# A DeltaNet and sliding-window layer: block stores from two queues, a block load that the queue waits for, and new places in the schedule

## The reference

```
g = cumsum(-exp(a_log) * softplus(a + dt_bias))
a_mat = strict(k_beta k^T) * decay
t_mat = inverse(I + a_mat)              # the triangular inverse
v_new = t_mat (v_beta - k_beta e^g S);  o = q e^g S + (q k^T * decay) v_new
S = S * e^g_tot + k_dec^T v_new
y = concat(rmsnorm(o) * silu(z), attention * silu(z_b)) @ w_out
out = LayerNorm(2^0.25 * x + y)
```

## Time and profile before

| | |
|---|---|
| median of 3 runs (lowest to highest) | 1247.62 us (1246.43 to 1248.07) |
| profiled execution, its own time | 1249.48 us |
| its span, first to last instruction | 1247.7 us |
| PE busy | 1149.6 us (92%) |
| DVE busy | 650.1 us (52%) |
| ACT busy | 505.5 us (41%) |
| POOL busy | 198.0 us (16%) |
| granted TensorE clock, mean | 0.970 |
| DMA engines' mean share | 45%, 147 GB/s |

### The profile page before, as it was taken

How to read it: one execution, slowest core, us unless ns; L and a number is a source line. 1 busy time by engine, 2 the same in 40 slices (tenths; PEclk the granted TensorE clock), 3 DMA queues, 4 the chain that set the end, 5 groups by cost and what they waited for, 6 DMA issues and landing times. The chain is left out here.

```text
span 1247.7 us, 19748 instructions
## 1 busy us (share of the span) xinstructions
PE 1149.6 (92%) x7340; PEld 900.9 (72%) x7340; DVE 650.1 (52%) x1996; ACT 505.5 (41%) x1475; POOL 198.0 (16%) x268
## 2 busy tenths in 40 slices
PE   4988989888999999999999999999899989899997
PEld 2766767666777868786786878777686868687776
DVE  3345554645355464646356364745437363636565
ACT  3363636363352625353352433336233534353220
POOL 4522323122210101023000101012100000000340
PEclk9998989898999999999999999999999999999999
DMA  6753745545572543632436362625244343522232
GB/s 212 287 191 123 252 164 161 179 136 153 161 237 102 164 160 104 211 127 78 150 132 193 124 192 79 201 84 172 85 165 157 110 137 110 168 79 61 94 109 84
DMA packets 63887, 183.57 MB, mean 147 GB/s; under 512 B 16240, under 2 KB 28976, under 8 KB 50480
## 3 DMA queue, kind: packets, MB, share of 16 engines
q1 hardware_dynamic: 63792, 182.32, 44.1%
HBM read 138.22 MB, written 44.07 MB: 146 GB/s over the span
## 5 line engine op out<-in xcount | busy, mean ns | idle before, releaser
L760 PE MATMUL bank<-xr,w 128*128 128x512 f32 x2496 | 684.8, 414 | 5.1 <-ACT conv_in L1091 3.2
L760 PEld LDWEIGHTS bank<-xr,w 128*128 128x128 f32 x2496 | 455.5, 193 | 108.5 <-issue 14.8
L733 POOL TENSOR_TENSOR x_tile<-x_tile,gain 128x256 f32<-128x256 f32 x40 | 28.1, 736 | 716.6 <-DVE x_tile L1484 716.6
L810 PE MATMUL bank<-wo,y_split 128*128 128x512 f32 x432 | 118.8, 409 | 0.0
L810 PEld LDWEIGHTS bank<-wo,y_split 128*128 128x128 f32 x432 | 76.2, 188 | 17.1 <-issue 1.9
L1410 DVE SCALAR_TENSOR_TENSOR kq<-conv_in,convw_all,kq 128x512 f32<-128x512 f32 x96 | 76.5, 796 | 3.4
L1332 ACT ACTIVATE blocks<-bank 128x128 f32<-128x128 f32 x64 | 17.8, 277 | 149.0 <-PE bank L1027 148.8
L1605 DVE TENSOR_TENSOR y_step<-blocks,y_cols 128x60 f32<-128x60 f32 (+14 forms) x240 | 49.7, 207 | 49.7 <-DMA blocks<-n_spill 42.0
L1227 ACT ACTIVATE score<-score,neg_max 128x256 f32<-128x256 f32 (+1 forms) x128 | 62.5, 490 | 16.8 <-DVE neg_max L1572 16.8
L1297 ACT ACTIVATE blocks<-bank 128x256 f32<-128x256 f32 (+1 forms) x64 | 24.4, 382 | 105.1 <-PE bank L974 73.7
L1692 DVE SCALAR_TENSOR_TENSOR t<-bank,cols_all,v_tok 128x128 f32<-128x128 f32 x64 | 22.3, 348 | 84.8 <-PE bank L1012 84.8
(11 more groups left out here) (214 smaller groups left out, 1762.1 us busy)
## 6 DMA issues: line engine op xcount, KB each, us to landing
w<-w_split SPq DMA_DIRECT2D x78, 1024.0 KB, 5.0
w_split<-w SPq DMA_DIRECT2D x26, 1024.0 KB, 4.9
blocks<-n_spill SPq DMA_DIRECT2D x16, 512.0 KB
y_spill<-y_out SPq DMA_DIRECT2D x30, 256.0 KB, 6.3
y_tile<-w_in SPq DMA_DIRECT2D x13, 512.0 KB, 6.1
x_tile<-w_in SPq DMA_DIRECT2D x13, 512.0 KB, 6.2
y_tile<-y_spill SPq DMA_DIRECT2D x12, 512.0 KB, 6.7
x_tile<-x SPq DMA_DIRECT2D x12, 512.0 KB, 5.6
```

The costliest lines, as they stand in the source:

```text
L733: nc.gpsimd.tensor_tensor(res[:, part], res[:, part], gain[:, part], ALU.mult).then_inc(scaled.sem, 1)
L760: ins = nc.tensor.matmul(bank[at % 2][:], w[:, turn % 3, wp, k, :], xr[:, xp, k], start=(step == 0), stop=(step == 3 * KT - 1))
L810: ins = nc.tensor.matmul(bank[at % 2][:], y_place(t)[:, yp, k], wo[:, k, wp, half * UNIT:(half + 1) * UNIT], start=(step == 0), stop=(step ...
```

## The change

1. `store_blocks` on SP issues five of the eight block stores; ACT issues the other three, after its squares of q and a wait for all of `n_t`.
2. `load_blocks(n)` comes directly after SP's stores, ahead of `load_decay(n + 1)`, and SP then waits for the blocks' landing before anything further (`load_x(s + 1, 3)`, weight loads, spills).
3. On ACT `eg_row` is made before the squares of k instead of after. A weight split (`w_hi`) that falls on a slot's last job is held until after ACT's block stores.
4. `silu` stands before chunk 2's square (the third chunk) instead of chunk 3's, where the gates are ready by then: in short and middle slots with n < 15. In long slots it stays.
5. In middle slots the job order is o0, bz, o1 instead of o0, o1, bz. `split_y` of the next tile moves from chunk 2 to chunk 3.
6. Places: `AT_VTOK` (L948) 0.13 to 0.16; `first` 0.47, 0.36, 0.42 to 0.49, 0.375, 0.44 (short, long, middle); `step0` and `step` as in the diff.

```diff
+SP_BLOCKS = 5
     if s == 1 or s == 2:
-        return ["q", "k", "v", "z", "o0", "o1", "bz", "bq"]
+        return ["q", "k", "v", "z", "o0", "bz", "o1", "bq"]
-AT_SCORES0, AT_VTOK, AT_TURNS0, AT_VALUES0 = 0.09, 0.13, 0.24, 0.31
+AT_SCORES0, AT_VTOK, AT_TURNS0, AT_VALUES0 = 0.09, 0.16, 0.24, 0.31
-        first = 0.47 if short else 0.36 if long else 0.42
+        first = 0.49 if short else 0.375 if long else 0.44
-        self.step0, self.step = (0.665, 0.082) if short else (0.6, 0.097) if long else (0.62, 0.092)
+        self.step0, self.step = (0.685, 0.077) if short else (0.605, 0.096) if long else (0.635, 0.088)
@@ sync
-                for g in range(P // BASE):
+                for g in range(SP_BLOCKS):
                 store_blocks(n)
+                load_blocks(n)
                 if i < AH - 1:
                     after(sp, pt_ready, n, 2)
                     load_decay(n + 1)
+                after(sp, blocks_in, n, 16)
                 if i == AH - 1 and 0 < s < SBS - 1:
                     after(sp, x_low_dve, s + 1, 1)
                     load_x(s + 1, 3)
-                load_blocks(n)
@@ scalar
+            held = []
+            def split_weight():
+                while held:
+                    w_hi(held.pop())
                 if at in W_AT and W_AT[at] + 3 < TILES_W:
-                    w_hi(W_AT[at] + 3)
+                    if at + 1 < len(JOBS) and JOBS[at + 1].n > max(job.n, -1) >= 0:
+                        held.append(W_AT[at] + 3)
+                    else:
+                        w_hi(W_AT[at] + 3)
             def slot(n):
+                after(act, g_row_in, n, 16)
+                after(act, resid_ready, n - 1, CH)
+                nc.scalar.activation(eg_row[:], decay[:], ACT.Exp).then_inc(eg_ready.sem, 1)
                 after(act, ktok_done, n, 1)
...
+                after(act, n_ready, n, CH)
+                for g in range(SP_BLOCKS, P // BASE):
+                    part = slice(g * BASE, (g + 1) * BASE)
+                    act.dma_start(n_spill[n, g].rearrange("t a c -> a t c"), n_t[part, :, part]).then_inc(n_stored.sem, 16)
+                split_weight()
                 after(act, small, n, 3)
...
-                after_jobs(n, at.step0)
+                after_jobs(n, min(at.step0, 0.66))
                 copy_turned(n, 1)
+                silu_before = CH - 2 if silu_at(n) - n < at.chunk(CH - 2) and n < SLOTS - 1 else CH - 1
                 for c in range(CH):
+                    if c == silu_before:
+                        after_jobs(n, max(at.chunk(c), silu_at(n) - n))
+                        if c < CH - 1:
+                            silu(n, True)
                     if c == CH - 1:
...
-                        silu(n, True)
+                        if silu_before == c:
+                            silu(n, True)
@@ vector
-                    if c == 2:
+                    if c == CH - 1:
                         if t is not None and i == AH - 2:
                             split_y(t + 1)
```

More of the change, by code:

```diff
@@ L1252, in slot @@
                 nc.scalar.activation(r_k[:], ln_ss[:, 0], ACT.Exp, scale=-0.5).then_inc(rk_ready.sem, 1)
-                after(act, g_row_in, n, 16)
-                after(act, resid_ready, n - 1, CH)
-                nc.scalar.activation(eg_row[:], decay[:], ACT.Exp).then_inc(eg_ready.sem, 1)
                 if i == 0:
@@ L1316, in slot @@
                 take(y_inv[low, :, high], half_tiles(bank[7])[low], 9)
-                after_jobs(n, at.step0)
+                after_jobs(n, min(at.step0, 0.66))
                 copy_turned(n, 1)
+                silu_before = CH - 2 if silu_at(n) - n < at.chunk(CH - 2) and n < SLOTS - 1 else CH - 1
                 for c in range(CH):
+                    if c == silu_before:
+                        after_jobs(n, max(at.chunk(c), silu_at(n) - n))
+                        if c < CH - 1:
+                            silu(n, True)
                     if c == CH - 1:
-                        after_jobs(n, max(at.chunk(c), silu_at(n) - n))
+                        after_jobs(n, at.chunk(c))
                         if t is not None and i == AH - 2:
```

## The result

The changed kernel takes 1262.41 us (median; 1261.24 to 1265.24), the kernel before 1247.15 (1246.43 to 1248.07) on the same chip: ratio 1.0119, 95% interval 1.0103 to 1.0135. It is slower by 15 us, where 1207 was forecast.

The account below looks back on a forecast made before the run. PE, busy 92% of the span, bounds it through waits and half clock. L963 saves 32.9, L948 5.0, added waits cost 13.8, net 24.1; clock saves 16.6: 40.7 off 1249.5, median 1207 us, range 1190 to 1229.

Parts of the forecast that it names:

- POOL beside DVE: POOL's tile scaling falls on n_t's chain, up to 1.7 us later but hidden; `store_tile` holds the block stores at most 0.6.
- Weight loads: On SP behind the blocks' landing: issued at 17.4 us into a slot, landing 5.1 at least, needed at 24.0, cost 0.
- Load alone: Block load with nothing beside it: lands in 5.0 us instead of 8.9 in slot 5; bounds 3.4 and 7.5.
- the rival that the load stays slow: Block load still takes 7.5 us, bringing gaps before the inverse's first matmul and half clock: +17, 1224 us; chance 0.20.
- Weights late: Weights landing in 12.0 us make PE wait in six middle and three short slots: 57 us, 1264 us; chance 0.06.
- The clock: PE's half-clock stretches after gaps: 9.5 left at 1.7 us each, 16.1 of 32.7 us, saving 16.6.
- L965's total: PE's waits for DVE's base inverse at the inverse's first matmul: from 44.8 to 11.9 us, saving 32.9.
- the margin of 2.7: In all six middle slots the base inverse ends 2.7 us before PE reaches the inverse's first matmul, so no gap.
- L897's 2.1: In slots 7 and 11 x is loaded behind the blocks' landing: new PE wait of 2.1 us per slot, bounds 0 and 4.
- Stores: Splitting eight block stores over SP and ACT lets the block load issue 1.4 us earlier per slot; bound 0 to 1.4.
- SiLU: `silu` in the third chunk makes PE wait 1.3 or 2.2 us in six short slots: 9.6 us added, bounds 0 and 14.
- SBUF's shared port: DVE and GpSimd lock the shared port for whole instructions; a base inverse step takes 0.17 us, 0.58 once POOL works.

Follow-up runs that it names:

- the decay experiment: The changed kernel with the decay load issued behind the landing of the blocks instead of beside it: 1269.65 us, ratio 1.0193 to the kernel before.

## Why the prediction was wrong

The sum had 40.7 us less; the profiled execution took 11.8 more: 52.5 us apart. The waits for weights (22.0 more than before), the clock (13.8 more than summed: 29.9 left of 32.7, where 16.1 had been said), L812 (6.2) and L970 (5.6 more) are 47.6 of them.

*The failed step* is in the part on POOL beside DVE: "SP's `store_tile`, waiting for it until about 8, holds the stores to at most 0.6 behind that", which the sentence before it takes as hidden under L953's bound. The time of `store_tile` was right (7.0 to 7.8), but it was priced by its wait alone. Behind it in SP's program come a weight load and in two slots two x loads, and all of that moves ahead of the 4 KB stores, which land 5.5 to 6.2 us after issue at the median in slot 5, where 1.0 behind the last issue had been taken. The block load left at 14.5 to 17.2 instead of 12.1. The edit of the order alone in the kernel before shows the same loss (1.0271), and with the old order in the changed kernel the load leaves at 12.1.

*The second failed step* follows from it: "Weight loads: issued at 17.4 instead of 11.9, needed at 24.0. Landing 5.1 at the least: just hidden, cost 0". They were issued at 21.6 to 24.4 in slots 5, 6, 9 and 10. Even where the first step is mended they are late, by 8.5 us in six slots, because the blocks land at 19.4 rather than 17.2. A margin of 1.5 us was called no cost.

*Load alone*: 5.0 forecast, 6.3 to 7.5 measured, 6.2 to 6.9 with nothing beside it. The step took the rate of all traffic, 174 GB/s, as the rate of the blocks alone. In the decay experiment the packets run for 3.9 us at 134 GB/s, where 3.0 had been taken, and 2.3 us of the 6.2 lie before and behind them, where 1.9 had been taken. The bound of 7.5 held it, and the rival that the load stays slow was nearly true, but that rival only moved L963 in its working, and left out the weights that wait for the same landing.

*Weights late*, at 0.06, is what happened, and its 1264 lies next to the result by another way: landing took 5.4 us and not 12; the issue was late. The range ended at 1229, so it left this case out.

*The clock*: 16.1 left was worked out with no stretch in any middle slot. Seven came there, with 25.6 us of PE work, so 12.8 us of cost: four behind waits for weights of 3.5 to 6.4 us, three behind L970's of 2.1 to 2.3. A stretch was priced at 1.7, though the prediction's own rows give 32.7/16 = 2.04; the eight stretches elsewhere cost 17.1, close to 16.1 because there were fewer of them than the 9.5 counted.

*L812*, 6.2 us in slots 7 and 11, is not in the sum. ACT's copy of za waits there for DVE's gate, a delay that the prediction had in slot 15 alone. It is 3.1 us in each, 1.8 with the old order, and 0.4 in the run with all eight stores on SP.

*What was right.* L1020: 9.6 forecast, 9.8 measured, 2.2 and 2.3 us in slots 0 and 1 and 1.3 in the other four, as worked out. L950: 1.6 forecast, 0.6 measured. n_t ends 3.3 to 3.4 us earlier in slots 1 and 2 (3.0 forecast) and 1.9 earlier in 3, 13 and 14 (1.7 forecast). Short slots issued the load at 10.5 to 11.1 as said (about 11). In the best version, where the order of jobs is the old one and the wait stays in short slots alone, the change gives 19 us (1245.8 to 1226.6).

*What was luck.* L965's total, 11.9 forecast and 12.7 measured, is made of other parts. Slots 0 to 2 have 4.6 us instead of 6.0: the blocks reach DVE 2 us later than forecast, and the base inverse is 1.6 to 1.9 us shorter, since POOL's split no longer lies on it, which the prediction had kept. Slot 3 has 3.9 instead of 1.5, slots 12 to 14 have 3.7 instead of 0, slots 7 and 11 none instead of 2.4, slot 15 0.6 instead of 2.0. That middle slots have no gap is owed to the late weights, which hold PE back: where these waits are nearly gone, in the best version, L966 waits 0.7 to 1.2 us in five of the six, so the margin of 2.7 was not there. L897's 2.1 in each of slots 7 and 11 came true as well, but x was issued at 23.4 us into slot 7 instead of 20.2, and PE came 3.1 later by L812.

*Stores*: 1.4 us of issue time each slot was within its own bound, but L953 sets the load just behind it, as the next step said, so little was left to save: all eight on SP cost 3.6 us by the ratios, not clear of noise. *SiLU*: its cost of 9.6 was right. It brings the first store in slots 1 and 2 from 8.2 to 6.2 us into the slot (9.5 before the change), two of the 3.0 us forecast for n_t, and that gave back about what it cost, no more.

*SBUF's shared port*: four DVE instructions took 3.02 us beside POOL's scaling and 1.14 without it, on n_t's chain. The Trainium skill (SBUF — State Buffer, "SBUF: two separate sides") has DVE and GpSimd take the port as an exclusive lock, and the trace agrees in direction. It is 1.9 us, close to the 1.7 forecast, and on n_t's chain it is not what decided. On the base inverse it matters more: 8.7 us beside POOL and 6.8 without it, in slots 0 to 2.

## What to carry to other kernels

When a job moves, follow what its result releases on an in-order queue: list every DMA between the new wait and the next small, urgent one, with its bytes, and charge the urgent one their transfer time. A wait for a landing holds back everything behind it: ask what that starts, and when it is needed. In short slots it was worth about 12 us here (0.9945 to 0.9851), most of it in slots 0 to 2, where it kept POOL's next split off DVE's base inverse. In the others, where PE wants the next weights about 4 us after the landing, it cost about 17 (0.9851 to 0.9989). When a total comes out as forecast, compare its parts before calling it right. A step whose cost is nothing by a margin of 1.5 us belongs in the range with its full price.

## What the runs showed of the hardware

Eight stores of 4 KB, issued after 2.5 MB on the same and on another queue, landed in 5.5 to 6.2 us at the median; in the slot where those had been issued earlier, in 1.8 to 2.1. A load of half a megabyte that reads each of eight parts sixteen times takes 6.2 to 6.9 us alone, at a mean of 83 GB/s, with the 16 DMA engines half busy while its packets run; it took 7.1 to 8.8 in the kernel before, so running it alone saves far less than its rate under traffic suggests. A weight load of a megabyte landed in 5.4 us at the median in the changed kernel. DVE's 30 dependent steps on the blocks take 6.8 us alone and 8.6 to 8.7 with some 2.9 us of POOL's work beside them.
